# A decoder trunk step: branch C's 16 low-rank gate columns as early fp32 products on four column strips

## The reference, cut to what matters

```python
h = rmsnorm(x, norm_pre)
p = split_cols(h @ w_in)      # ... c_q 512, c_k 512, c_v 1024, c_r 16, c_g 1024, ...
# branch C (gated linear attention), r = p["c_r"], 16 columns:
log_a = log_sigmoid(r @ gla_w_up + gla_b_up) / 16      # (288,16) @ (16,512)
# ... chunked recurrence with log_a, c_q, c_k, c_v; then all five branches A..E:
merged = sum over branches of sigmoid(h @ w_merge) * (branch * silu(gate)) @ w_branch
y = x + rmsnorm(merged @ w_out, norm_post)
```

## Time and profile before

| what | value |
|---|---|
| median of 3 runs | 1893.56 us (1892.53 to 1895.47) |
| the profiled execution, first to last instruction | 1893.8 us |
| TensorE matmul busy | 1863.6 us (98%) |
| TensorE weight loads (beside matmuls) | 1818.2 us (96%) |
| DVE / ACT / POOL busy | 1254.4 / 908.6 / 420.6 us |
| HBM read / written | 321.15 / 26.92 MB |
| mean granted TensorE clock | 0.995 |

### The profile page before, as it was taken

How to read it: one execution, slowest core, us unless ns; L and a number is a source line. 1 busy time by engine, 2 the same in 40 slices (tenths; PEclk the granted TensorE clock), 3 DMA queues, 4 the chain that set the end, 5 groups by cost and what they waited for, 6 DMA issues and landing times.

```text
span 1893.8 us, 39170 instructions
## 1 busy us (share of the span) xinstructions
PE 1863.6 (98%) x16424; PEld 1818.2 (96%) x16424; DVE 1254.4 (66%) x2227; ACT 908.6 (48%) x1335; POOL 420.6 (22%) x712
## 2 busy tenths in 40 slices
PE   7999999999999999999999999999999999999996
PEld 6999999999999999999999999999999999999996
DVE  8555568777766667666788788786556555444544
ACT  7533335554554544445556566664333333433442
POOL 5778778688500000000000000001000000000000
PEclk9999999999999999999999999999999999999998
DMA  6887765545554454545454555556555544655552
GB/s 247 302 283 253 250 236 185 181 170 180 204 174 158 174 192 145 193 146 198 158 167 160 176 180 169 164 163 232 171 168 180 182 155 150 206 168 167 167 168 84
DMA packets 92816, 350.62 MB, mean 185 GB/s; under 512 B 11904, under 2 KB 12304, under 8 KB 88032
## 3 DMA queue, kind: packets, MB, share of 16 engines
q1 hardware_dynamic: 77040, 280.53, 43.9%
q0 software_dynamic: 11568, 47.50, 7.1%
q10 hardware_dynamic: 4032, 20.09, 2.9%
HBM read 321.15 MB, written 26.92 MB: 184 GB/s over the span
## 4 chain that ended last, share of the span: by engine, by line
PE 95%; DVE 3%; ACT 1%; issue 1%; DMA 0%; SPq 0%; ACTq 0%; DVEq 0%
PE ps L1727 93%; DVE w_lo L1095 1%; DMA raw<-in_w 0%; PE ps L2059 0%; DVE acc L1089 0%; DVE acc L1092 0%; ACT g_t L609 0%; ACT w_hi L609 0%; PE ps L1916 0%; DVE xc L1101 0%; DVE g_X L1095 0%; PE ps L1949 0%; SPq L355 0%; DVE br_lo L1101 0%; DVE norm L1715 0%
## 5 line engine op out<-in xcount | busy, mean ns | idle before, releaser
L1727 PE MATMUL ps<-h_hi,w_hi 128*128 128x288 f32 x2960 | 882.7, 299 | 5.1 <-ACT h_hi L609 2.7
L1095 DVE TENSOR_TENSOR w_lo<-raw,w_hi 128x1024 fp32r<-128x1024 f32 x522 | 653.6, 1263 | 338.8 <-ACT w_hi L609 336.1
L1727 PE MATMUL ps<-h_hi,w_lo 128*128 128x288 f32 x2960 | 872.2, 295 | 0.0
L1727 PE MATMUL ps<-h_lo,w_hi 128*128 128x288 f32 x2960 | 867.0, 295 | 0.0
L609 ACT ACTIVATE w_hi<-raw 128x1024 fp32r<-128x1024 f32 x522 | 548.2, 1057 | 513.0 <-PE ps L1727 460.7
L1727 PEld LDWEIGHTS ps<-h_hi,w_hi 128*128 128x128 f32 x2960 | 555.5, 188 | 12.9 <-issue 8.8
L1727 PEld LDWEIGHTS ps<-h_hi,w_lo 128*128 128x128 f32 x2960 | 556.3, 188 | 1.2
L1727 PEld LDWEIGHTS ps<-h_lo,w_hi 128*128 128x128 f32 x2960 | 556.2, 188 | 0.3 <-DVE h_lo L1095 0.2
L1727 PE MATMUL ps<-br_hi,w_hi 128*128 128x288 f32 x640 | 192.1, 300 | 0.0
L1727 PE MATMUL ps<-br_hi,w_lo 128*128 128x288 f32 x640 | 188.8, 295 | 0.0
L1727 PE MATMUL ps<-br_lo,w_hi 128*128 128x288 f32 x640 | 188.3, 294 | 0.0
(11 more groups left out here) (386 smaller groups left out, 2290.1 us busy)
## 6 DMA issues: line engine op xcount, KB each, us to landing
raw<-in_w SPq DMA_DIRECT2D x522, 512.0 KB, 3.8
w_scratch<-st_wide POOLq DMA_DIRECT2D x72, 128.0 KB, 3.5
a_w<-w_scratch POOLq DMA_DIRECT2D x8, 1152.0 KB, 7.4
acc<-in_kc ACTq DMA_DIRECT2D x8, 1024.0 KB, 7.7
vc<-in_vc ACTq DMA_DIRECT2D x8, 1024.0 KB, 5.9
c_S<-in_gla POOLq DMA_DIRECT2D x4, 1024.0 KB, 7.4
out_gla_s<-c_S POOLq DMA_DIRECT2D x4, 1024.0 KB, 5.1
h_S<-in_hgrn POOLq DMA_DIRECT2D x8, 512.0 KB, 4.3
```

The source lines that it names most:

```text
L1095: return dve.tensor_tensor(out, a, b, ALU.subtract)
L1727: return pe.matmul(out, a, b, start=start, stop=stop)
```

## The change

- ("cr", 0) leaves `ORDER`: 520 units are left, and every later block changes its PSUM bank and its slot.
- The 16 columns, padded to 32, come as `w_rank` (128 x 16 x 32 fp32, 256 KB) by a DMA that ACT issues after the squares of x. It lies in the space of `prob`.
- TensorE multiplies it in plain fp32 with the normalised `acc`, between the h_hi part and the h_lo part of the first two blocks: 16 matmuls, tile k on column strip k mod 4 of PSUM bank 5, so that each strip of 32 partitions sums four tiles.
- ACT copies that bank to `c_r_early` (in the space of `sq`) after the kc load, and at the end of branch E's fourth head to `c_r`, which has 1152 bytes per partition of its own.
- The up matrix is laid out four times, on partitions 0, 32, 64 and 96 (16 rows each, zeros between), so that the one product `c_z` with 128 rows also adds up the four strips. It is 256 KB now.
- `c_z` of head 0 stands before `h("ck", 0)`, as for the other heads; ACT's copy `g_r` and its wait are gone.
- Five semaphores on which nobody waited are merged into `copied`.

```diff
-    order += [("cr", 0)]
...
+        c_r_early = sq[:, KT - 1]
...
+        w_rank = prob[:, 0:2].rearrange("p a m -> p (a m)").rearrange("p (k c) -> p k c", c=32)
...
+        c_r = sb("c_r", [P, T], F32, r_st)
...
-        g_wu = sb("g_wu", [GLA_RANK, 4, P], F32, v_st)
-        g_r = sb("g_r", [GLA_RANK, T], F32, v_st)
+        g_wu = sb("g_wu", [P, 4, P], F32, v_st)
...
                 f(sq[:, k:k + n], acc[:, k:k + n], ACT.Square, "squared")
+            load(w_rank, t["w_rank"], "w_rank_landed")
             upto(1)
...
             act.wait_ge(S("split"), 4)
+            act.wait_ge(S("c_ranks"), 1)
             load(kc[:, 0], t["kc"][0, :, 0], "kc_landed")
+            f(c_r_early, ps[:, 5, 0:T], ACT.Copy, "c_r")
...
                         f(vm[:], ps[:, 6].rearrange("p (a b) -> p a b", a=2), ACT.Copy, "e_vm")
+                        if i == 3:
+                            act.wait_ge(S("c_r"), 1)
+                            f(c_r[:], c_r_early, ACT.Copy, "c_r")
...
-            u0 = UNIT["cr", 0]
-            upto(u0 + 4)
+            upto(UNIT["ck", 0] + 2)
             act.wait_ge(S("g_params"), 48)
-            wait_block(act, "cr", 0)
             act.wait_ge(S("tab_kept"), 128)
-            f(g_r[:], ps[0:GLA_RANK, bank(("cr", 0)), 0:T], ACT.Copy, frees(("cr", 0)))
...
-            upto(UNIT["cr", 0] + 4)
+            upto(UNIT["ck", 0] + 2)
...
+            pe.wait_ge(S("w_rank_landed"), 16)
+            pe.wait_ge(S("normed"), KT)
+            for k in range(KT):
+                j = 32 * (k % 4)
+                ins = mm(ps[j:j + 32, 5, 0:T], w_rank[:, k], acc[:, k], k < 4, k >= KT - 4)
+            sg(ins, "c_ranks")
...
-            h("cr", 0)
             for i in range(4):
                 if i == 0:
-                    h("ck", 0)
                     pe.wait_ge(S("g_params"), 48)
-                    wait_taken(pe, "cr", 0)
+                    pe.wait_ge(S("c_r"), 2)
...
-                sg(mm(ps[:, 7, 0:T], g_wu[:, i], g_r[:]), "c_z")
-                if i:
-                    h("ck", i)
+                sg(mm(ps[:, 7, 0:T], g_wu[:, i], c_r[:]), "c_z")
+                h("ck", i)
...
+    low_rank = np.zeros((D_MODEL, 32), np.float32)
...
+    rank_up = np.zeros((4, 32, 4, P), np.float32)
+    rank_up[:, :GLA_RANK] = g["gla_w_up"].reshape(GLA_RANK, 4, P)
```

More of the change, by code:

```diff
@@ L196, in build @@
         m_rstd = sd[:, 0:N_MEM]
+        r_st = ExitStack()
+        c_r = sb("c_r", [P, T], F32, r_st)
         d_st = ExitStack()
@@ L277, in build @@
         g_st.close()
+        r_st.close()
         a_st = ExitStack()
@@ L755, in _ @@
                     wait_block(act, "dx", 0)
-                    f(d_xp[:, 3:3 + SEQ], ps[:, bank(("dx", 0)), 0:SEQ], ACT.Copy, "d_xp")
+                    f(d_xp[:, 3:3 + SEQ], ps[:, bank(("dx", 0)), 0:SEQ], ACT.Copy, "copied")
                     f(d_xs[:, :, 3:3 + NT], by_seq(ps[:, bank(("dx", 0))]), ACT.Copy, frees(("dx", 0)))
@@ L779, in _ @@
                     wait_block(act, "dx", i)
-                    f(d_xp[:, 3:3 + SEQ], ps[:, bank(("dx", i)), 0:SEQ], ACT.Copy, "d_xp")
+                    f(d_xp[:, 3:3 + SEQ], ps[:, bank(("dx", i)), 0:SEQ], ACT.Copy, "copied")
                     f(d_xs[:, :, 3:3 + NT], by_seq(ps[:, bank(("dx", i))]), ACT.Copy, frees(("dx", i)))
@@ L882, in _ @@
                 f(g_t[:, 0], ps[:, 7, 0:T], ACT.Abs, "c_abs", bias=bias)
-                f(g_t[:, 2], ps[:, 7, 0:T], ACT.Identity, "c_zb", bias=bias)
+                f(g_t[:, 2], ps[:, 7, 0:T], ACT.Identity, "copied", bias=bias)
                 act.wait_ge(S("c_abs"), i + 1)
@@ L939, in _ @@
                 act.wait_ge(S("g_rstd"), i + 4)
-                f(g_t[:, 2], src, ACT.Copy, "b_zb")
+                f(g_t[:, 2], src, ACT.Copy, "copied")
                 f(g_t[:, 0], src, ACT.Abs, frees(("hf", i)))
@@ L951, in _ @@
                 act.wait_ge(S("b_kz"), i + 1)
-                f(g_k[:], g_k[:], ACT.Exp, "b_kexp")
+                f(g_k[:], g_k[:], ACT.Exp, "copied")
                 f(g_t[:, 1], g_t[:, 0], ACT.Exp, "b_em")
@@ L2166, in layout @@
         at += width
-    low_rank = np.zeros((D_MODEL, P), np.float32)
+    low_rank = np.zeros((D_MODEL, 32), np.float32)
     low_rank[:, :GLA_RANK] = win["c_r"]
+    rank_up = np.zeros((4, 32, 4, P), np.float32)
+    rank_up[:, :GLA_RANK] = g["gla_w_up"].reshape(GLA_RANK, 4, P)
     wb = {short: blocks(win[name]) for short, name in NAMES.items()}
-    wb.update(ek=blocks(g["w_mem_k"]), ev=blocks(g["w_mem_v"]), cr=blocks(low_rank), glu=blocks(g["s5_w_glu"]),
+    wb.update(ek=blocks(g["w_mem_k"]), ev=blocks(g["w_mem_v"]), glu=blocks(g["s5_w_glu"]),
               out=blocks(g["w_out"]))
@@ L2196, in layout @@
         "lb": tiles(g["hg_lb_logits"]),
-        "w_up": g["gla_w_up"].reshape(GLA_RANK, 4, P),
+        "w_up": rank_up.reshape(P, 4, P), "w_rank": low_rank.reshape(KT, P, 32).swapaxes(0, 1),
         "gla": g["state_gla"].transpose(1, 2, 0, 3), "hgrn": g["state_hgrn"].transpose(1, 2, 0, 3),
```

## The result

The changed kernel takes 1890.62 us (median of 11 runs, 1886.28 to 1893.65), the kernel before 1893.89 us (11 runs beside them; one of these took 6844.14 us, for which the record has no cause, and the ratio leaves it out). The ratio is 0.9982 with a 95% interval of 0.9973 to 0.9990: 3.3 us faster, between 1.9 and 5.1. The forecast was 5.15 less. The two profiled executions lie 4.4 us apart (spans of 1893.8 and 1889.4). A profiled execution's time is its span plus about 1.7 us (1891.09 for the one after), so the one before took some 1895.5, the slowest of the three that were shown; the comparison rests on the medians.

What follows compares the result with a forecast made beforehand. TensorE's issue intervals were taken to bound the kernel (matmuls 98% of the span). -6.4 + 2.3 - 0.7 - 0.35 = -5.15 us took 1893.8 to 1888.65, and 0.24 over the median gave 1888.4; 8 in 10 range 1886.6 to 1891.2.

Steps and rivals of the forecast that it cites:

- What goes, -6.4: Head of branch C: removing block cr takes 48 matmuls at 0.133 us each from TensorE's stream, -6.4 us.
- the wait at the third C block: TensorE's wait for a w_lo there should go because c_z's chain starts earlier, -0.35 us (bounds 0 and -0.37).
- What comes, +2.3 for the 32 records: Near 26 us: 16 fp32 products on four overlapping strips cost 2.3 us, judged by the similar eq_own products.
- rival C: Strips overlap partly: loads in line, insertion 5.7, total -1.75 us (3%); or matmuls not overlapping, 7.8, total +0.35 (3%).
- The cover, -0.7 on it: Behind the strips, two waits of TensorE at the h_lo and w_lo matmuls (0.37 and 0.34) hide 0.7 us.
- Rival A: At the start, w_rank's transfer delays the second raw and the reciprocal by up to 0.65 us: total -4.5, 1889.1; 12%.
- c_z, "128 rows for 16 change nothing": Product with the up matrix in branch C: TensorE's cost stays the same, 0.24 us a record with either row count.
- "Eleven us of slack, nothing" for g_params: Head of branch C: up matrix issued at 506.6, landing at 512, wanted at about 523.3, so no cost.
- "Under 1%" for a late parameter: Head of branch C: chance that c_z waits for c_r or its parameters, both said to be set over 10 us before.
- The B stage, "which I have at nothing": A new wait in the C or B stage because banks and slots changed places was put at nothing.
- Base time: The sum started from the profiled execution's 1893.8 us, taken as 0.24 us over the median of the runs.

Runs made afterwards that it cites:

- experiment 3: Changed kernel with c_z of head 0 behind the block ck again, other heads as they are: 1890.61 us, 0.9981 of the kernel before.
- Experiment 10: Changed kernel with all 16 fp32 products on one column strip and c_z with 32 rows: 1898.37 us, 1.0017 of the kernel before.
- experiment 1: Kernel before with the up matrix and g_r on 128 rows for 16, zeros in the rest: 1892.45 us, 0.9991 of the kernel before.
- 2: Changed kernel without the 16 fp32 products, c_r copied from another bank, so branch C's gates are wrong: 1887.54 us, 0.9972 of the kernel before.
- 11: Changed kernel with the removed block's 1 MB kept in the weight array but skipped, so later weights keep their addresses: 1891.43 us, 0.9987 of the kernel before.
- experiment 12: Changed kernel with the up matrix loaded early on ACT's queue and the removed block's 1 MB kept in memory but skipped: 1887.65 us, 0.9965 of before.
- experiment 6: Changed kernel with the up matrix loaded on ACT's queue at the end of branch E, not by GpSimd: 1887.79 us, 0.9968 of the kernel before.
- 4: Changed kernel again, unchanged, for a second profiled execution: 1890.92 us, 0.9983 of the kernel before.
- 8: Changed kernel with the up matrix loaded early on ACT's queue and two DVE splits made earlier (branches D and B): 1888.41 us, 0.9967 of before.

## Why the prediction was right, and where not

The sign and the range of 8 in 10 held; the gain is 3.3 us for 5.15 forecast, and 1890.6 lies outside the 1887.6 to 1889.4 that the forecast gave itself. The main mechanism, a block's 6.4 us against some 2 us of strips, is as predicted. Step by step:

- **What goes, -6.4.** The block went with all its matmuls: in the profiles -7.2 at the head of branch C, which is 6.4, the wait at the third C block (0.35 forecast, 0.37 gone; 0.58 back in experiment 3), and 0.4 from c_z.
- **What comes, +2.3 for the 32 records.** 2.08 measured; the row of eq_own was the right neighbour. Experiment 10 shows what the four strips do: 7.88 without them. It lies at the price of the full-width rows, the forecast's 7.8, as in the second case of rival C. That kernel is slower than before by 0.0017, 3.2 us, where rival C had +0.35: it also has the dearer c_z, a wait of 2.6 for the up matrix with low clock behind it, and the wait in branch B. The Trainium skill (TensorE: Matmul & The Clock Gate, The mechanism) lets loads overlap with matmuls in flight only when their row group differs; that would have put 32 loads of 0.106, 3.4 us, in line. The measured 2.08 us for loads and matmuls together doesn't agree with it for column strips. Nor does the stream around them, as the page of the kernel before could have told: its full-width loads last 0.188 us each, and the matmuls, one load to each, follow every 0.133.
- **The cover, -0.7 on it.** The block eg starts 1.79 later instead of 1.6: the strips started 0.06 later and 0.35 of the 0.7 was hidden. The other half stands also in the kernel after, where DVE's third w_lo ends 1.9 us ahead of eg (33.05), so TensorE wasn't waiting for it. I had read as idle time what is left at these two places without a wait; why the interval is longer where one kind of group follows another isn't shown.
- **Rival A.** The issue came at 9.64, the landing at 17.0, and nothing of the start moved. The Trainium skill's sentence on rings served in turn (DMA: Bandwidth & Descriptors, Queues, rings and completion order) agrees: w_rank was issued behind SP's queued units and the memory tokens, and it landed ahead of the tokens, at 17.8 and 20.2.
- **c_z, "128 rows for 16 change nothing".** Wrong by 0.34 to 0.40 a head, 1.4 us in favour of the change (experiment 1). The two rows compared were read for the two records of a product by themselves; the cost is at its borders. With 16 rows it starts 0.23 us behind the matmul ahead and the next block 0.67 behind its start, with 128 rows 0.13 and 0.27.
- **"Eleven us of slack, nothing" for g_params.** This is the step that failed. It rested on one execution's issue at 506.6, and in six of eleven profiles it is 11 to 15 us later. The kernel before wants the matrix at 536 and can't see that; without the block it is wanted at 521 to 528, and the four late ones (2, 3, 10, 11) wait 2.6 to 4.6 us, three of them with a stretch of low clock that costs 1.4 to 2.2 more. Together that is 3.7 to 6.7 us, 4.8 on the mean. At about one execution in two it takes some 2 to 3 us off the mean gain (an estimate), and it would explain why the changed kernel's runs spread over 7.4 us and those of experiment 12 over 1.8 (11 runs and 5). That the load's place costs time is shown by experiments 6, 11 and 12: with that one load moved the ratio is 0.9968 and 0.9965, 6.0 and 6.6 us below before, and 12 passes a late set-up without the wait that 11 has. How often the changed kernel itself meets a late set-up isn't shown; both of its profiles are early. "Under 1%" for a late parameter was the worst number of the prediction.
- **The B stage, "which I have at nothing".** A wait with the exchange of places was named as what would show it wrong. The wait came, and took 1.2 us of the gain in the pair of profiles, 0.5 to 3.7 in the ten; that the exchange of places is its cause isn't shown.
- **Base time.** The sum was taken from the span, as if that were a run's time, and the profiled execution called 0.24 over the median; it was 1.7 + 0.24 over. Against the median the number comes out the same, 1893.56 - 5.15 = 1888.4.

Together: 5.15 + 1.4 (c_z) - 0.2 (start) - 1.2 (branch B) = 5.15 for an execution with an early set-up. That this is the forecast's number again is luck: two terms that it didn't have, 1.4 for c_z and -1.2 for branch B, cancel. If about half of the executions lose 3.7 to 6.7 of it, 2 to 3 us less on the mean, some 2 to 3 are left for the 3.3 (1.9 to 5.1) measured. How much the waits at 176 and 308 us add, and in which execution, isn't settled.

The version that beats both kernels is experiment 6 (and 12, the same within 0.0003): 1887.8 us, 0.9968 [0.9956, 0.9981], against the kernel before; its interval overlaps the changed kernel's, and it is the comparison of 12 with 11 that sets the two apart.

## What to carry to other kernels

A margin read from one profile is that profile's margin: before a wait is moved forward to just behind another engine's long work, look at when that work ends in more executions, and of the edited kernels too, and load small parameters far ahead, where it is free. A few narrow products on column strips cost a quarter of their price in series. When a block is taken out of a stream with rotating buffers, a new wait can turn up far behind; look for chains of small transfers that end just in time.

## What was not expected of the hardware

- An fp32 product with 16 rows between fp32r ones costs 0.34 to 0.40 us more on TensorE than the same one with 128 rows, the other 112 being zero: 1.27 for 0.87 us from the matmul ahead to the third behind. With 32 rows it is 1.27 as well.
- GpSimd's 500 us of set-up end in one of two clusters, 11 to 15 us apart, six of fourteen profiles in the early one. What chooses between them isn't known.
- TensorE's clock was granted at half for 3.4 us behind waits of 2.0 us (311.3 to 314.7, before), 2.6 (532.9 to 536.3, in 10) and 3.3 (525.3 to 528.7, in 11), and for 6.8 us from the last part of a wait of 2.7 (310.7 to 317.6, after) and of 4.6 (523.2 to 530.0, in 2) on. In branch B it was so for 3.4 us, beginning 2.4 us behind a wait of 2.2 (in 4) and 2.7 behind one of only 1.0 (in 8), with 64 products of 32 rows and 72 columns between. Waits of 2.0 (at 311, in 6) and of 3.7 (at 526, in 3) were followed by none. Where it could be measured, 3.4 us of it cost 1.4 to 1.6 us.
